# Scattering one pair later, scattering the last pair on two row groups, and the last norm by products with a diagonal

## The reference, cut to what matters

```
def moe_ffn(x, router_w, router_b, w_gate, w_up, w_down):
    """Shared router; pick top-1 expert group (sum of its top-2 probs), then top-2 experts in it."""
    ...
    y = jnp.zeros((B * T, D), f32)
    for e in range(N_EXPERTS):
        h = jax.nn.silu(xt @ w_gate[e]) * (xt @ w_up[e])
        y = y + combine[:, e:e + 1] * (h @ w_down[e]).astype(f32)
    ...
    x = layer_norm(ALPHA * x + moe_ffn(x, ...), ln2_g, ln2_b)
```

## Time and profile before

| | |
|---|---|
| median of 3 runs | 1694.95 us (1694.47 to 1695.22) |
| the profiled execution | 1694.34 us, span 1692.6 us |
| mean granted TensorE clock | 0.992 of full |
| PE busy | 94% of the span |
| DVE busy, ACT busy | 41%, 23% |
| read from HBM | 537.73 MB |

### The profile page before, as it was taken

The page is one execution under the profiler, slowest core; times in us unless marked ns, Lnnn a source line. Parts: engine busy times, 40 slices in busy tenths (PEclk is TensorE's granted clock), DMA queues, the critical chain, the costliest instruction groups (busy, mean ns, idle before and its releaser), DMA issues.

```text
span 1692.6 us, 23705 instructions
## 1 busy us (share of the span) xinstructions
PE 1595.0 (94%) x10374; PEld 1075.0 (64%) x10374; DVE 686.4 (41%) x991; ACT 386.5 (23%) x398; POOL 43.1 (3%) x79
## 2 busy tenths in 40 slices
PE   8999999999999999999999998998998988988995
PEld 8999999999999999983433432433334324324432
DVE  6547678648585565545510110300201101202706
ACT  5454555523354332330000000000000000000000
POOL 2000000012000000000000000000000000000000
PEclk9999999999999999999999999999999999999998
DMA  8675566579656759979999999999999999999996
GB/s 241 185 224 151 150 177 172 150 196 330 195 163 179 234 182 307 277 277 375 423 389 430 427 428 428 429 429 428 429 427 429 428 429 429 429 428 429 427 416 226
DMA packets 252719, 545.86 MB, mean 322 GB/s; under 512 B 6080, under 2 KB 219152, under 8 KB 228320
## 3 DMA queue, kind: packets, MB, share of 16 engines
q1 hardware_dynamic: 245888, 527.06, 82.6%
q0 software_dynamic: 4640, 15.47, 2.9%
q10 hardware_dynamic: 2112, 2.16, 0.4%
HBM read 537.73 MB, written 6.95 MB: 322 GB/s over the span
## 4 chain that ended last, share of the span: by engine, by line
PE 84%; DMA 11%; DVE 3%; ACT 1%; issue 1%; DVEq 0%; POOL 0%; ACTq 0%
PE bank L892 18%; PE bank L957 13%; PE bank L608 12%; PE bank L609 12%; PE bank L610 12%; DMA ring_high<-wu 9%; PE bank L867 5%; PE bank L1013 3%; PE bank L651 2%; DMA ring_high<-wd 1%; PE bank L947 1%; ACT xt L1187 1%; DMA reg_uv<-x_t 1%; DVE reg_pk L1550 0%; PE bank L1007 0%
## 5 line engine op out<-in xcount | busy, mean ns | idle before, releaser
L610 PE MATMUL bank<-x_hi,w_lo 128*128 128x264 f32 x1216 | 344.3, 283 | 0.0
L608 PE MATMUL bank<-x_hi,w_hi 128*128 128x264 f32 x1200 | 343.4, 286 | 0.4 <-DVE w_lo L1228 0.4
L609 PE MATMUL bank<-x_lo,w_hi 128*128 128x264 f32 x1200 | 340.0, 283 | 0.0
L1228 DVE TENSOR_TENSOR w_lo<-ring_low,w_hi 128x2048 fp32r<-128x2048 f32 x107 | 244.8, 2288 | 154.3 <-ACT w_hi L1060 153.9
L892 PE MATMUL bank<-ring_low,reg_pk 128*64 128x512 f32 x1008 | 224.8, 595 | 22.4 <-DMA ring_low<-wu 18.6
L1060 ACT CAST w_hi<-ring_low 128x2048 fp32r<-128x2048 f32 x107 | 203.6, 1903 | 143.1 <-PE bank L610 91.2
L892 PE MATMUL bank<-ring_high,reg_pk 128*64 128x512 f32 x1024 | 225.3, 593 | 7.3 <-DMA ring_high<-wu 6.6
L610 PEld LDWEIGHTS bank<-x_hi,w_lo 128*128 128x128 f32 x1216 | 228.0, 187 | 0.0
L608 PEld LDWEIGHTS bank<-x_hi,w_hi 128*128 128x128 f32 x1200 | 226.1, 188 | 1.6 <-issue 0.8
L609 PEld LDWEIGHTS bank<-x_lo,w_hi 128*128 128x128 f32 x1200 | 226.2, 189 | 0.1
L892 PEld LDWEIGHTS bank<-ring_low,reg_pk 128*64 128x64 f32 x1008 | 69.6, 137 | 172.3 <-issue 132.2
(11 more groups left out here) (339 smaller groups left out, 1769.1 us busy)
## 6 DMA issues: line engine op xcount, KB each, us to landing
ring_low<-w_in SPq DMA_DIRECT2D x76, 1024.0 KB, 5.8
ring_high<-wg SPq DMA_DIRECT2D x34, 2048.0 KB, 24.0
ring_low<-wu SPq DMA_DIRECT2D x33, 2048.0 KB, 26.7
ring_high<-wd SPq DMA_DIRECT2D x32, 2048.0 KB, 27.3
ring_low<-wd SPq DMA_DIRECT2D x31, 2048.0 KB, 18.5
ring_low<-wg SPq DMA_DIRECT2D x30, 2048.0 KB, 33.6
ring_high<-wu SPq DMA_DIRECT2D x30, 2048.0 KB, 24.1
ring_low<-wo SPq DMA_DIRECT2D x16, 1024.0 KB, 6.9
```

Of the source, the lines that this page charges most:

```text
L608: pe.matmul(out, hi[k], of_hi[:, k, :], start=(k == 0), stop=False)
L609: pe.matmul(out, hi[k], of_lo[:, k, :], start=False, stop=False)
L610: mm = pe.matmul(out, lo[k], of_hi[:, k, :], start=False, stop=(k == kk - 1))
L1228: dve.tensor_tensor(lo_of(q), raw_of(q), hi_of(q).bitcast(F32), ALU.subtract).then_inc(lo_ready, 1)
```

## The change

1. A pair's scatter moves: in the pairs of the fixed list it is done in the next pair, behind that pair's first expert (gate and up). DVE's adds move along. The transposes of the hidden rows are their own function: those of the first expert come behind the scatter, those of the second between the third and fourth part of the gather. They write to bank 0 (first expert) and bank 2 (second), not to bank 6.
2. Last pair: the first expert's part of the scatter is done alone (`scatter_first`, 64 rows of the contraction), one product behind each unit of the second expert. The second expert's part uses column halves of the down result as two row groups (`pick_t2` holds its choice matrix twice, on partitions 0 to 63 and 64 to 127), with products of 256 columns, in the middle of the next unit. ACT copies both halves in one instruction. The last unit comes in two DMAs.
3. Last norm: gain and bias come as two rows for each quarter by small DMAs of POOL; PE spreads the gain by products with a selector (`row_out`) during the last pair, and ACT copies it. Behind the last scatter, PE writes the bias into banks the same way, with 16 filler products between them, DVE does (x - mean) * gain, PE multiplies that with a diagonal of 1/std on top of the bias, ACT copies the result and SP writes it. ACT issues the sample rows' DMAs.

The core of the diff (names of semaphores, the branch for further pairs, and the places of buffers are left out):

```
+KEEP_WARM_LAST = 16
...
+                        if m < UNITS - 1:
+                            sp.dma_start(by_block(ring_slot(s)), src).then_inc(landed[s], 16)
+                        else:
+                            sp.dma_start(by_block(ring_slot(s))[:, 0:4, :], src[:, 0:4, :]).then_inc(landed[s], 16)
+                            sp.dma_start(by_block(ring_slot(s))[:, 4:8, :], src[:, 4:8, :]).then_inc(half_in, 16)
...
+                        if last and a and part + q:
+                            scatter_first(i, 4 * part + q - 1)
...
+            def scatter_first(i, b):
...
+                    tt, nn = divmod(b - 1, 4)
+                    if b > 1:
+                        pe.wait_ge(first_ev, b - 1)
+                    pe.matmul(psum[6 + b % 2][:, :], pick_t[0:CAP, P * tt:P * tt + P], ob[0:CAP, 512 * nn:512 * nn + 512], start=True, stop=True).then_inc(first_mm, 1)
...
+            def row_out(bank, c, a):
+
+                rows = slice(32 * c, 32 * c + 2)
+                return pe.matmul(bank[:, :], ident[rows, 32 * c + a:32 * c + a + 1].broadcast_to([2, P]), ln2_rows[rows, :], start=True, stop=(a == 0))
...
             def down_last(i):
...
+                        if c == 3 and k == 4:
+                            pe.wait_ge(half_in, 16)
...
+                        if c and k == 3:
+                            scatter_last(i, c - 1)
                     mm.then_inc(w_used, 1)
-                    if c:
-                        scatter_last(i, c - 1)
+                    if c == 0:
+                        pe.wait_ge(rows_in, 16 * 8)
+                        gain_out().then_inc(gain_mm, 1)
                 scatter_last(i, 3)
...
                 for tt in range(2):
-                    if c:
-                        pe.wait_ge(sc_ev, i * N_SC + 2 * (c - 1) + tt + 1)
-                    pe.matmul(psum[6 + tt][:, :], pick_t[:, P * tt:P * tt + P], ob[:, 512 * c:512 * c + 512], start=True, stop=True).then_inc(sc_mm, 1)
+                    for half in range(2):
+                        rows = slice(64 * half, 64 * half + 64)
+                        mm = pe.matmul(psum[6 + half][:, 256 * tt:256 * tt + 256], pick_t2[rows, P * tt:P * tt + P], ob[rows, 512 * c:512 * c + 256],
+                                       start=True, stop=True)
+                mm.then_inc(sc_mm, 2)
...
-            def pair(i, first=False, last=False):
+            def pair(i, first=False, last=False, own=False):
                 expert(i, 0, not first, last, first)
+                if not first and not own:
+                    scatter(i - 1)
+                hid_transposed(i, 0)
                 pick_transposed(i, first)
+                if last:
+                    pick_twice(i)
                 down(i, 0, not last, first)
-                expert(i, 1)
+                expert(i, 1, True, last)
                 if last:
                     down_last(i)
                 else:
-                    gather(i + 1)
+                    gather(i + 1, range(3))
+                    hid_transposed(i, 1)
+                    gather(i + 1, range(3, 4))
                     down(i, 1)
-                    scatter(i)
+                    if own:
+                        scatter(i)
...
+            for c in range(3):
+                row_out(psum[c], c, 1)
+            for _ in range(KEEP_WARM_LAST):
+                pe.matmul(psum[3][:, 0:P], ones[:, :], ones[:, :], start=True, stop=True)
+            row_out(psum[3], 3, 1)
...
+                pe.wait_ge(y_mul, n + 1)
+                pe.matmul(bank[:, :], spread[:, tt, :], acc[:, tt, 512 * c:512 * c + 512], start=False, stop=True).then_inc(y_mm, 1)
...
+            for tt in range(2):
+                act.activation(spread[:, tt, :], ident[:, :], ACT.Identity, scale=mv[:, tt, 3:4]).then_inc(spread_ready, 1)
...
+                act.wait_ge(y_mm, n + 1)
+                act.copy(acc[:, tt, 512 * c:512 * c + 512], bank[:, :]).then_inc(y_ready, 1)
```

More of the change, by code:

```diff
@@ L455, in _ @@
             with sp.If(pairs > 0):
+                sp.wait_ge(gain_ev, 4)
                 with sp.Fori(0, pairs) as j:
@@ L586, in _ @@
             pool.nop().then_inc(quarter_ready, 1)
+            pool.wait_ge(hid_ready, 2 * NPAIR - 1)
+            for c in range(4):
+                for a, par in enumerate((ln2g, ln2b)):
+                    pool.dma_start(ln2_rows[32 * c + a:32 * c + a + 1, :], par[512 * c:512 * c + 512].unsqueeze(0)).then_inc(rows_in, 16)
             pool.wait_ge(outs, 16)
@@ L869, in gather_part, with gather @@
                 mm.then_inc(g_mm, 1)
-            def gather(p):
+            def gather(p, parts):
                 pe.wait_ge(picked, p + 1)
-                for r in range(4):
+                pe.wait_ge(pick_ev, p)
+                for r in parts:
                     gather_part(p, r)
@@ L926, in expert @@
                             gather_part(0, q + 2)
-                        if last and part == 0:
+                        if last and not a and part == 0:
                             residual(q)
@@ L1182, in pair @@
                         act.activation(hid_out, by_two(psum[2 * a][:, :]), ACT.Silu).then_inc(silu, 1)
+                    act.wait_ge(hid_tr, i * 2 + (a + 1))
+                    act.copy(hidt.rearrange("p j f s -> p (j f s)"), psum[2 * a][:, :]).then_inc(hid_ev, 1)
                     if a == 0:
@@ L1185, in pair @@
                         act.copy(pick_t, psum[7][:, 0:2 * P + 32]).then_inc(pick_ev, 1)
-                    act.wait_ge(hid_tr, i * 2 + (a + 1))
-                    act.copy(hidt.rearrange("p j f s -> p (j f s)"), psum[6][:, :]).then_inc(hid_ev, 1)
+                    if last and a == 0:
+                        act.wait_ge(pick_tr2, 1)
+                        act.copy(pick_t2, psum[6][:, 0:2 * P + 32]).then_inc(pick_ev2, 1)
                     if last and a:
@@ L1658, in residual, with pair @@
                 link(dve.tensor_tensor(acc_s[quad, :], acc_s[quad, :], part1[quad, 2, :], ALU.add))
-            def pair(i, last=False):
+            def pair(i, last=False, own=False):
                 weigh(i)
@@ L1665, in pair @@
                 hidden(i, 0)
+                if not own:
+                    add_scattered(i - 1)
                 if not last:
@@ L1680, in pair @@
                     result(i, 1)
-                    add_scattered(i)
+                    if own:
+                        add_scattered(i)
             weigh(0)
@@ L1708, in _ @@
                 with dve.Fori(0, pairs) as j:
-                    pair(j + NPAIR)
+                    pair(j + NPAIR, own=True)
                 for tt in range(2):
@@ L1716, in _, with centred @@
                 dve.wait_ge(again, 1)
+                for tt in range(2):
+                    dve.bn_aggr(mv[:, tt, 0:2], stat[:, tt, 0:4, :].rearrange("p n s -> p (n s)")).then_inc(again, 1)
+                dve.wait_ge(again, 3)
+                dve.wait_ge(gain_ev2, 4)
             ms = mv[:, 2, :]
-            for tt in range(2):
-                dve.bn_aggr(mv[:, tt, 0:2], stat[:, tt, 0:4, :].rearrange("p n s -> p (n s)")).then_inc(l_var, 1)
+            dve.wait_ge(gain_ev, 4)
+            def centred(n):
+                tt, c = divmod(n, 4)
+                cols = slice(512 * c, 512 * c + 512)
+                dve.scalar_tensor_tensor(out=acc[:, tt, cols], in0=acc[:, tt, cols], scalar=mv[:, tt, 0:1], in1=ln2_gain[:, cols],
+                                         op0=ALU.subtract, op1=ALU.mult).then_inc(y_mul, 1)
+            dve.wait_ge(l_var, 3)
+            centred(0)
+            dve.wait_ge(l_std, 2)
+            dve.reciprocal(mv[:, 0:2, 3], mv[:, 0:2, 2]).then_inc(l_inv, 1)
+            centred(1)
             dve.wait_ge(sc_ev, pairs * N_SC + NPAIR * N_SC)
@@ L1764, in _ @@
             dve.scalar_tensor_tensor(out=acc_s, in0=acc_s, scalar=ms[:, 3:4], in1=ln2q[:, 1, :], op0=ALU.mult, op1=ALU.add).then_inc(ys_ready, 1)
-            for n in range(5, 8):
-                centred(n)
-                scaled(n - 1)
-            scaled(7)
 def kernel(**inputs):
```

204 lines of the change are left out of this document (130 added, 74 removed).

## The result

The changed kernel takes 1696.28 us (median of 20 runs, 1692.81 to 1698.02), the kernel before 1693.05 us in 20 runs (1688.46 to 1695.86). The ratio is 1.0023 [1.0016, 1.0029]: **slower by 0.23%**, where the forecast was 1691.7, a gain of 0.2%. Both kernels differ by some microseconds from run to run. Part of this is seen in the profiles: at the start of the kernel the clock is at half speed for 3.4 us in the profile of before (12.5 to 15.9) and for 6.8 us in that of the changed kernel (11.5 to 18.3), long before any line that the change touches. So I compare stretches inside the span, not only ends.

The account below looks back on a forecast made before the run. Weights bound the middle pairs. The span was to go from 1692.6 to 1667.9 + 21.9 = 1689.8, 2.8 less, giving 1692.15 and, with starts overcharged, a forecast of 1691.7 us; range 1686.5 to 1698.

Parts of the forecast that it names:

- The stop at 870 to 880: Expert stage, pair 0's scatter: weight stream stops with all slots full, losing 3.7 us; scattering a pair later removes this.
- lead at U: At U, the landing of pair 6's last weight unit: weights forecast to land 3.7 us earlier than before.
- PE late in the last pair: Last pair: PE no longer waits for weights, so 3.4 of the 3.7 us are paid back as PE work.
- E: End of the last product with weights: forecast 1667.9, only 0.25 us better than 1668.15 before.
- the scatter step: Middle of a late last-pair unit: four 256-column products in two row groups, taken as 1.0 us (bounds 0.9 and 1.9).
- rival 1: Last pair and norm: row groups don't run side by side, 9.8 us more, 1701.5, slower; chance 0.13.
- plan load 0.5: PE behind the last scatter, ahead of the bias rows: loading the plan was counted as 0.5 us.
- rival 2: Last norm: PE's clock falls to half over the products, up to 8.6 us more, 1693.4 to 1700; chance 0.10.
- E + 8.3: Behind E: PE's bias rows and fillers end and the norm's products start 8.3 us after E.
- The last unit in halves buys nothing: End of the last pair: both halves land (1657.8 and 1660.5) before PE comes to them.
- the removal of the broadcasts: DMA queue behind the weights: the 2 MB of broadcast parameters were there when first read, so removal is worth nothing.
- the moved transposes: Hidden-row transposes: cover SiLU, multiply and copy (2.8 us), worth nothing in a pair bound by weights, but useful in the last.

Follow-up runs that it names:

- experiment 1: Changed kernel without PE's load of the plan and PE's branch over the further pairs: 1689.93 us, ratio 0.9980 to the kernel before.
- experiment 7: Changed kernel with the further pairs left out of the body of PE's branch, load and branch kept: 1691.03 us, ratio 0.9986 to the kernel before.
- experiment 11: Changed kernel with the last unit of weights in one DMA instead of two, one execution: 1698.09 us.
- experiment 9: Changed kernel with the scatter back in its own pair, all else as changed: 1701.91 us, ratio 1.0041 to the kernel before.
- experiment 10: Changed kernel with PE's plan load ahead of the last pair, 8 fillers ahead of the branch and 8 behind: 1692.32 us, ratio 0.9990 to before.
- experiment 6: Changed kernel with PE's plan load ahead of the last pair, bias rows and 16 fillers ahead of the branch: 1693.99 us, ratio 1.0011 to before.
- experiment 3: Changed kernel with PE's load of the plan moved ahead of the last pair, branch left in place: 1694.50 us, ratio 1.0005 to before.
- experiment 2: Changed kernel without the 16 filler products behind the last scatter: 1693.19 us, ratio 1.0001 to the kernel before.
- experiment 8: Changed kernel without PE's branch and without the 16 fillers: 1691.58 us, ratio 0.9989 to the kernel before.

## Why the prediction was wrong

**What held.** The stop at 870 to 880 and its end: lead at U 4.0 (3.7 forecast). PE late in the last pair: E at 1666.45 against 1667.9, by the very pieces that were counted: down at 1594.94 (1596.2), the scatter product between units 1.05 (1.15), four gain rows 1.07 (1.0), the scatter step 1.06 (1.0). Whether a drain is in this step, which the prediction took at 0.3 us, no run separates. Row groups run side by side: four 256-column products on two groups in 1.06, four 512-column products on four groups in 1.07; rival 1 is out, and the block L906 had shown it. DVE and ACT were ready in time: the diagonal at about E + 7.4.

**What failed is one term behind E: "plan load 0.5"** for PE. It measured 3.81. The term is right for the load (0.49) and has nothing for the branch behind it (3.50). 0.5 is what DVE and ACT need at the same place (0.45 and 0.56), but PE jumps over the code of whole further pairs; with a short body PE needs 0.49. The kernel before has the same branch, and its trace had the price: 3.48 us (L1034). It cost nothing there because PE had nothing to do behind the branch until DVE's statistics came (PE idle from 1673.0 to 1676.83, the branch over at 1675.2). The change put 8 us of PE work right behind it. The stall pushed that work back by 3.3 us more than counted. That the measured time lies inside the stated range, up to 1698, is luck: the range was that wide for rivals 1 and 2, slow row groups and a half clock over the norm, and neither of them had the stall in it.

**The second failure follows from the first.** Behind 3.8 us of idle PE the clock fell, as rival 2 had it, but over the fillers instead of over the products: 5.40 against 3.8, another 1.6. In experiments 1 and 7, the same products without the stall, it stayed at 1.00. Together 4.9 of the 5.3 us between E + 8.3 and E + 13.6. The products and the output behind them took 0.5 us more than counted. Without the branch the same marks are E + 8.07 and E + 22.4, against 8.3 and 21.9 forecast.

**Smaller ones.** "The last unit in halves buys nothing" was wrong by 1 us (experiment 11), and the removal of the broadcasts was not worth nothing: it lets the small loads in beside the last unit. The whole lead was put on the scatter's later place, and the moved transposes were called worth nothing where weights bound the pair. Pair 0, where the stream stops because PE is behind, is not such a pair: the transposes alone bring 2.7 of the 4 us there (experiment 9). The lead itself is not sharp to more than about 1.5 us: with the same order of work up to U, U - S is 767.3 to 767.5 where the clock fell near 789 us (changed kernel, experiments 1, 10, 11) and 765.7 to 766.4 in the seven profiles where it did not. Before has such a fall too.

**Where the gain goes.** From U to the end, before takes 167.9 us, the changed kernel 174.0, without the branch 168.6, with the old norm 167.7, with the first part alone 169.3 (of which the half clock in its last pair is 1.5). So the second and third part of the change bring nothing even without the stall, and the whole gain to be had is the lead of the stream, 4 us: 0.9977 with the first part alone, 0.9976 with the first two. These two are the lowest ratios of all; experiment 1, which leaves out the path for further pairs, is at 0.9980, within their intervals.

## What to carry to other kernels

A stall of a sequencer (a branch over much code, a load of a value) is free only while its engine has nothing to do behind it. Before moving work to an engine, look in its waits for "issue" at that place, ask for the line of the branch itself, and take the number of that engine, not that of its neighbours. When the clock is to be kept up by fillers, count the time until the engine gets its first instruction behind a branch, not only the time until its data are there.

## What was not expected of the hardware

- A branch over a long body takes PE's sequencer 3.35 to 3.92 us (ten profiles), over a short body 0.21, and ACT and DVE 0.05 and 0.07. Of this PE stands idle 2.8 us with the value already loaded and 3.8 to 4.2 with the load right ahead; 0.49 with the short body. With 4 to 6 us of work queued ahead of it (experiments 10 and 6) 0.5 to 0.7 us remain: the branch began only 3.0 to 3.1 us before the queue was empty.
- Four products with two rows each, on four row groups and 512 columns wide, take 1.07 us together, as long as one alone (1.05).
- The clock, once fallen, did not come back after a fixed time. With PE busy for all or nearly all of the time it stayed at half for 3.4 us (changed kernel, experiment 3), for 6.8 (experiments 2, 9, 11) and for 10.2 us (6, 8). In experiment 6 it fell with no more than 0.72 us of idle PE, behind a stretch with two-row products; with 8 fillers behind that gap it didn't (experiment 10, one profile each).
